# Expert weights in 16 KB rows, and a tail that joins, normalises and stores one token tile at a time

## What is computed

```python
# x: 264 tokens x 1024; h = rmsnorm(x)
logits = xt @ w_router + b_router
top_vals, top_idx = lax.top_k(logits, TOP_K)          # 4 of 32 experts a token
gates = jax.nn.softmax(top_vals, axis=-1)
...
gate, up = jnp.split(xb @ w_gate_up[e] + b_gate_up[e], 2, axis=-1)   # 1024 -> 2 x 1024
gate = jnp.minimum(gate, SWIGLU_LIMIT)
up = jnp.clip(up, -SWIGLU_LIMIT, SWIGLU_LIMIT)
act = gate * jax.nn.sigmoid(SWIGLU_ALPHA * gate) * (up + 1.0)
y = act @ w_down[e] + b_down[e]                                      # 1024 -> 1024
...
x = x + sum over a token's 4 experts of gates * y
y = rmsnorm(x, norm_final)
```

## Time and profile before

| | |
|---|---|
| median of 3 runs | 1428.51 us (1427.23 to 1429.93) |
| the profiled execution: time | 1428.02 us |
| its span | 1426.0 us |
| TensorE busy | 1331.8 us, 93% |
| VectorE, ScalarE, GpSimd busy | 374.5, 248.6, 60.4 us |
| moved | 515 MB in 84,586 packets, 361 GB/s over the span |

### The profile page before, as it was taken

The page is one execution under the profiler, slowest core; times in us unless marked ns, Lnnn a source line. Parts: engine busy times, 40 slices in busy tenths (PEclk is TensorE's granted clock), DMA queues, the critical chain, the costliest instruction groups (busy, mean ns, idle before and its releaser), DMA issues.

```text
span 1426.0 us, 19764 instructions
## 1 busy us (share of the span) xinstructions
PE 1331.8 (93%) x7729; PEld 632.0 (44%) x7729; DVE 374.5 (26%) x836; ACT 248.6 (17%) x403; POOL 60.4 (4%) x101
## 2 busy tenths in 40 slices
PE   6999959979996999999999999999999999999995
PEld 5666547647753433433343333333343333333333
DVE  3001684221225222212222222122221222212223
ACT  2010212220214111111111111111111111111112
POOL 2022220210000000000000000000000000000000
PEclk9999979989998999999999999999999999999998
DMA  9998574376883799999999999999999999999993
GB/s 341 371 360 333 192 264 179 121 255 245 319 359 136 302 424 422 421 421 422 422 422 421 422 422 422 423 421 423 422 422 422 422 423 422 422 421 423 422 422 121
DMA packets 84586, 515.13 MB, mean 361 GB/s; under 512 B 8451, under 2 KB 9563, under 8 KB 34608
## 3 DMA queue, kind: packets, MB, share of 16 engines
q1 hardware_dynamic: 77648, 493.69, 85.5%
q0 software_dynamic: 6576, 20.25, 4.4%
q10 hardware_dynamic: 336, 0.82, 0.2%
HBM read 511.21 MB, written 47.52 MB: 392 GB/s over the span
## 4 chain that ended last, share of the span: by engine, by line
PE 65%; DMA 20%; DVE 6%; SPq 6%; issue 2%; ACT 1%; POOL 0%; DVEq 0%; ACTq 0%
PE psum L573 61%; DMA weights<-in_w_gate_up 19%; SPq L445 5%; PE psum L576 4%; DVE qk L1384 1%; DMA weights<-in_w_mem_kv 1%; DMA weights<-in_cache_mem_kv 1%; DVE weights L1085 1%; DVE samp L1089 0%; DVE weights L1081 0%; DVE samp L1083 0%; DVE pair L1229 0%; ACT th L1539 0%; POOL weights L516 0%; DVE x L1409 0%
## 5 line engine op out<-in xcount | busy, mean ns | idle before, releaser
L573 PE MATMUL psum<-weights,wsp 128*64 128x512 f32 x2048 | 491.8, 603 | 15.0 <-DMA weights<-in_w_gate_up 14.3
L573 PE MATMUL psum<-weights,merged 128*64 128x512 f32 (+2 forms) x1152 | 272.8, 595 | 1.5 <-issue 1.5
L573 PEld LDWEIGHTS psum<-weights,wsp 128*64 128x64 f32 x2048 | 127.3, 136 | 267.1 <-issue 176.9
L1354 DVE TENSOR_TENSOR hT<-psum,hT 128x264 f32<-128x264 f32 x264 | 101.8, 428 | 529.6 <-PE psum L573 529.5
L573 PE MATMUL psum<-hT,weights 128*128 128x264 f32 x704 | 164.8, 391 | 1.2 <-DVE pair L1229 0.9
L573 PEld LDWEIGHTS psum<-weights,merged 128*64 128x64 f32 (+2 forms) x1152 | 89.6, 140 | 156.4 <-issue 148.3
L573 PEld LDWEIGHTS psum<-hT,weights 128*128 128x128 f32 x704 | 133.4, 191 | 28.8 <-DVE pair L1229 4.5
L1600 ACT COPY bT<-psum 128x264 f32<-128x264 f32 x33 | 12.5, 380 | 484.2 <-PE psum L576 484.2
L573 PE MATMUL psum<-bT,merged 64*128 64x264 f32 x528 | 94.2, 434 | 1.1 <-ACT merged L1619 0.7
L1384 DVE TENSOR_SCALAR qk<-psum,lowest 128x512 f32<-128x512 f32 x64 | 48.1, 751 | 162.7 <-PE psum L573 159.2
L573 PEld LDWEIGHTS psum<-bT,merged 64*128 64x128 f32 x528 | 39.8, 184 | 106.7 <-issue 103.9
(11 more groups left out here) (267 smaller groups left out, 721.9 us busy)
## 6 DMA issues: line engine op xcount, KB each, us to landing
weights<-in_w_gate_up SPq DMA_DIRECT2D x256, 1024.0 KB, 26.2
weights<-in_w_down SPq DMA_DIRECT2D x128, 1024.0 KB, 25.0
out<-in_cache_win_kv SPq DMA_DIRECT2D x8, 4094.0 KB, 20.9
weights<-in_w_in SPq DMA_DIRECT2D x13, 2048.0 KB, 12.5
out<-in_cache_win_kv SPq DMA_DIRECT2D x2, 4088.0 KB, 19.1
weights<-in_cache_mem_kv POOLq DMA_DIRECT2D x14, 512.0 KB, 6.4
weights<-in_cache_win_kv POOLq DMA_DIRECT2D x42, 128.0 KB, 4.5
weights<-in_w_mem_kv SPq DMA_DIRECT2D x2, 2048.0 KB, 18.0
```

The lines of the kernel that those rows point to most:

```text
L573: return nc.tensor.matmul(out, lhsT, rhs, start=start, stop=stop, **kw)
L1354: V.tensor_tensor(acc[:, c, :], p_a[j % 2][part], acc[:, c, :], ALU.add).then_inc(s_acc, 1)
```

## The change

Three things, all in the expert stage and behind it:

- A slot is 2 MB and there are six of them. Chunks 0 to 3 are 256 rows of w_gate_up (two neighbouring rows of 8 KB a partition), chunks 4 and 5 are 512 rows of w_down (four neighbouring rows of 4 KB a partition). A partition gets 16 KB in one piece. SyncE's waits and TensorE's `s_used` follow: one per slot.
- With it the gather takes its 128 stationary columns at a step of 2 (bf16), and the turns of h at a step of 4 (f32).
- The last expert is not scattered into `acc`. `acc` is turned into PSUM by f32 matmuls against the identity (`turn_sums`), and the last expert's rows are added on top, gate values as the stationary operand and `y_tok` as the moving one (`last_expert`). Three PSUM areas hold the three tiles. Join, square, root, scaling and store are done for each tile by itself, and ScalarE makes a first square root right after the loop. The counters of the loop drop the odd 33rd step.

```diff
-CHUNKS = KD + KD // 2
+GU, DN = 4, 2
+CHUNKS = GU + DN
+SLOT = 4 * D
...
-            return k if k < 4 else 4 + (k - 2) % 8
+            return k if k < 2 else 2 + (k - 1) % 4
...
-            return weights_at[:, n * 2048:(n + 1) * 2048]
+            return weights_at[:, n * SLOT:(n + 1) * SLOT]
...
             def chunk_dyn(e, k):
                 s = chunk_slot(k)
-                if k < KD:
-                    src = I["w_gate_up"][0, bass.ds(e, 1), k * P:(k + 1) * P, :].rearrange("e p c -> p (e c)")
-                    dst = chunk_view(k)
+                if k < GU:
+                    src = I["w_gate_up"][0, bass.ds(e, 1), k * 2 * P:(k + 1) * 2 * P, :].rearrange("e (p j) c -> p (e j c)", p=P)
                 else:
-                    r = (k - KD) * 2 * P
-                    src = I["w_down"][0, bass.ds(e, 1), r:r + 2 * P, :].rearrange("e (p j) c -> p (e j) c", p=P)
-                    dst = chunk_view(k).rearrange("p (j c) -> p j c", j=2)
-                sp.dma_start(dst, src).then_inc(s_chunk_in[s], 16)
+                    src = I["w_down"][0, bass.ds(e, 1), (k - GU) * 4 * P:(k - GU + 1) * 4 * P, :].rearrange("e (p j) c -> p (e j c)", p=P)
+                sp.dma_start(chunk_view(k), src).then_inc(s_chunk_in[s], 16)
...
-                    sp.wait_ge(s_job, last_job[{6: 17, 8: 18, 10: 19, 4: 20}[chunk_slot(k) // 2 * 2]])
+                    sp.wait_ge(s_job, last_job[{3: 17, 4: 18, 5: 19, 2: 20}[chunk_slot(k)]])
...
                     if k == CHUNKS - 1:
-                        sp.wait_ge(s_y, n33 + 1)
-                    elif k == KD - 1:
+                        sp.wait_ge(s_y, n32)
+                    elif k == GU - 1:
                         sp.wait_ge(s_gu, n32 * 2)
-                    elif k < KD:
+                    elif k < GU:
                         sp.wait_ge(s_used, n32 * USED + (k + 1 - USED))
                     else:
                         sp.wait_ge(s_used, n32 * USED + (k - USED))
                     chunk_dyn(e, k)
...
-                    ks, out = slice(k * P, (k + 1) * P), p_x[:, k * SLOTS:(k + 1) * SLOTS]
+                    first = k // 2 * 2 * P + k % 2
+                    ks, out = slice(first, first + 2 * P - 1, 2), p_x[:, k * SLOTS:(k + 1) * SLOTS]
...
-                        pe.wait_ge(s_chunk_in[chunk_slot(k)], n32 * 16 + 16)
-                        w = chunk_view(k)
+                        if k % 2 == 0:
+                            pe.wait_ge(s_chunk_in[chunk_slot(k // 2)], n32 * 16 + 16)
+                        w = chunk_view(k // 2)[:, (k % 2) * 2 * D:(k % 2 + 1) * 2 * D]
...
-                        if k < KD - 1:
+                        if k % 2 == 1 and k < KD - 1:
                             last.then_inc(s_used, 1)
...
-                            first = k // 2 * 2 * P + k % 2
-                            last = turn(p_hT[:, k, :], h_tok[:, first:first + 2 * P - 1:2], P)
+                            first = k // 4 * 4 * P + k % 4
+                            last = turn(p_hT[:, k, :], h_tok[:, first:first + 4 * P - 3:4], P)
...
-                        c = KD + k // 2
+                        c = GU + k // 4
...
-                        if k % 2 == 0:
+                        if k % 4 == 0:
                             pe.wait_ge(s_chunk_in[chunk_slot(c)], n32 * 16 + 16)
-                        w = chunk_view(c)[:, (k % 2) * D:(k % 2 + 1) * D]
+                        w = chunk_view(c)[:, (k % 4) * D:(k % 4 + 1) * D]
                         last = column_pair(p_y, actT[:, k, :], w[:, 0:512], w[:, 512:1024], k == 0, k == KD - 1)
                         if k == KD - 1:
                             last.then_inc(s_y, 1)
-                        elif k % 2 == 1:
+                        elif k % 4 == 3:
                             last.then_inc(s_used, 1)
-                last33 = b * (E + 1) + E
-                pe.wait_ge(s_ytok, last33 + 1)
-                pe.wait_ge(s_gT, last33 + 1)
-                for j in range(PAIRED):
-                    scatter(last33, j)
...
-            pe.wait_ge(s_accout, 1)
-            for t, (t0, tn) in enumerate(TILES):
-                w = wide[t % 2]
-                if t == 2:
-                    pe.wait_ge(s_finT, 1)
+            joined = (psum[:, 0:1024], psum[:, 1024:2048], wide[1])
+            def turn_sums(t):
+                t0, tn = TILES[t]
                 for k in range(KD):
-                    last = turn(w[0:tn, k * P:(k + 1) * P], acc[:, k, t0:t0 + tn], P)
-                last.then_inc(s_finj, 1)
+                    mm(joined[t][0:tn, k * P:(k + 1) * P], acc[:, k, t0:t0 + tn], ident, k % 4 == 0, False, skip_group_check=True)
+            def last_expert(t):
+                t0, tn = TILES[t]
+                mm(joined[t][0:tn, 0:512], gT[0:SLOTS, t0:t0 + tn], y_upper, False, True, skip_group_check=True)
+                mm(joined[t][0:tn, 512:1024], gT[SLOTS:2 * SLOTS, t0:t0 + tn], y_lower, False, True,
+                   skip_group_check=True).then_inc(s_finj, 1)
+            pe.wait_ge(s_accout, 1)
+            turn_sums(0)
+            turn_sums(1)
+            pe.wait_ge(s_ylast, 1)
+            last_expert(0)
+            last_expert(1)
+            turn_sums(2)
+            last_expert(2)
...
-            for t, (_, tn) in enumerate(TILES):
+            def join(t):
+                tn = TILES[t][1]
                 dve.wait_ge(s_finj, t + 1)
-                V.tensor_tensor(x1[0:tn, t, :], x1[0:tn, t, :], wide[t % 2][0:tn, :], ALU.add).then_inc(s_finT, 1)
-            rms_scale(stat[:, 28:31], D, 14)
-            dve.wait_ge(s_rt, 6)
-            seq(V.reciprocal(stat[:, 28:31], stat[:, 28:31]))
-            dve.wait_ge(s_gfin_in, 16)
-            for t, (_, tn) in enumerate(TILES):
+                V.tensor_tensor(x1[0:tn, t, :], x1[0:tn, t, :], (psum[:, 0:1024], psum[:, 1024:2048], wide[1])[t][0:tn, :],
+                                ALU.add).then_inc(s_finT, 1)
+            def root(t):
+                rms_scale(stat[:, 28 + t:29 + t], D, 12 + t)
+            def finish(t):
+                tn = TILES[t][1]
+                dve.wait_ge(s_rt, 6 + t)
+                seq(V.reciprocal(stat[:, 28 + t:29 + t], stat[:, 28 + t:29 + t]))
                 V.scalar_tensor_tensor(x1[0:tn, t, :], x1[0:tn, t, :], stat[0:tn, 28 + t:29 + t], gfin[0:tn, :], ALU.mult,
                                        ALU.mult).then_inc(s_fin, 1)
+            join(0)
+            join(1)
+            root(0)
+            join(2)
+            root(1)
+            dve.wait_ge(s_gfin_in, 16)
+            finish(0)
+            root(2)
+            finish(1)
+            finish(2)
...
-                    act.wait_ge(s_y, n33 + 2)
+                    act.wait_ge(s_y, n32 + 1)
                     A.copy(y_tok, p_y).then_inc(s_ytok, 1)
+                act.wait_ge(s_ytok, b * E + (E + 1))
...
-            for t, (_, tn) in enumerate(TILES):
+            act.sem_inc(s_ylast, 1)
+            A.activation(stat[:, 39:40], stat[:, 39:40], ACT.Sqrt)
+            def square(t):
+                tn = TILES[t][1]
                 act.wait_ge(s_finT, t + 1)
                 squares(stat[0:tn, 28 + t:29 + t], x1[0:tn, t, :], xr[0:tn, t, :])
-            act.wait_ge(s_ms, 6)
-            A.activation(stat[:, 28:31], stat[:, 28:31], ACT.Sqrt).then_inc(s_rt, 1)
+            def root(t):
+                act.wait_ge(s_ms, 6 + t)
+                A.activation(stat[:, 28 + t:29 + t], stat[:, 28 + t:29 + t], ACT.Sqrt).then_inc(s_rt, 1)
+            square(0)
+            square(1)
+            root(0)
+            square(2)
+            root(1)
+            root(2)
```

More of the change, by code:

```diff
@@ L190, in sem @@
             return ctx.enter_context(nc.semaphore(name))
-        weights_at = sb("weights", [P, CHUNKS * 2048])
-        scratch = weights_at[:, 0:4 * 2048]
-        ring = weights_at[:, 4 * 2048:CHUNKS * 2048]
+        weights_at = sb("weights", [P, CHUNKS * SLOT])
+        scratch = weights_at[:, 0:2 * SLOT]
+        ring = weights_at[:, 2 * SLOT:CHUNKS * SLOT]
         def block_view(name, p=P):
@@ L469, in _ @@
             with sp.Fori(1, E) as e:
[L470 removed]
+                one_expert(e, e)
             sp.wait_ge(s_done["posm"], 1)
@@ L868, in gather, with scatter @@
                 last.then_inc(s_gath, 1)
-            def scatter(n33, j):
+            def scatter(n32, j):
                 if j >= 2:
-                    pe.wait_ge(s_acc, n33 * KD + 2 * (j - 1))
+                    pe.wait_ge(s_acc, n32 * KD + 2 * (j - 1))
                 cs = slice(j * P, (j + 1) * P)
@@ L910, in one_pass @@
                                 last.then_inc(s_gu, 1)
-                        if k < KD - 1:
+                        if k % 2 == 1 and k < KD - 1:
                             last.then_inc(s_used, 1)
                         if k == 1:
-                            pe.wait_ge(s_ytok, n33 + 1)
-                            pe.wait_ge(s_gT, n33 + 1)
+                            pe.wait_ge(s_ytok, n32 + 1)
```

(26 more changed lines are left out.)

37 lines of the change are left out of this document (15 added, 22 removed).

## The result

| | before | after |
|---|---|---|
| median | 1429.21 us (1427.23 to 1429.93, 4 runs) | 1410.23 us (1409.70 to 1411.58, 4 runs) |
| the profiled execution: time | 1428.02 us | 1409.84 us |
| its span | 1426.0 us | 1408.0 us |
| packets | 84,586 | 56,939 |

The ratio of the times is 0.9876, with a 95% interval of 0.9858 to 0.9893. The two spans differ by 18.0 us, the forecast was 11.1. Three stretches of the span show where that comes from. Their bounds are the first and the last copy of y_tok, since each starts as soon as a down product ends.

What follows compares the result with a forecast made beforehand. Transfers were taken to bound the late experts (29.82 us each against TensorE's 28.31). Terms -14.2 + 2.2 + 0 + 0.9 = -11.1 us, from 1428.02, gave 1417 us; own range 1411 to 1423, outer range 1410 to 1431.

Steps and rivals of the forecast that it cites:

- What bounds the kernel: Expert stage: TensorE needs 28.31 us an expert, weight transfers set 29.82 once the starting stock is eaten, around expert 14.
- Rows of 16 KB, -14.2: Weight transfers: 9.9 ns a row, so fewer, larger rows give 429 GB/s and 29.34 us an expert, -14.2 us.
- The rival of an unchanged rate: Weight transfers: a limit behind the rows keeps the rate at 422 GB/s, time 1431.1 us; chance 0.11.
- that of a third of the row cost: Weight transfers: the skill's packet cost of 3.5 ns holds, gain about 5 us, time 1426 us; chance 0.06.
- Larger slots, +2.2: End of the expert stage: TensorE ends 4.5 us behind the last landing instead of 2.3, +2.2 us once.
- Startup, 0 give or take 1.5: First experts with six slots: expert 1's weights complete about 503.5 us, as before; 0, give or take 1.5 us.
- The steps, 0: Stationary loads of gather (step 2, bf16) and turns (step 4, f32): no dearer than before, 0 us.
- Both rivals that slowed TensorE down: Expert stage loads: turns slowed, 1424.5 us, chance 0.07; gather slowed, 1455.5 us at twice as long, chance 0.08.
- The tail, +0.9: Down product's end to span's end: 24.6 us instead of 23.7, the 3.9 us loop exit following the down product.
- 24 at 0.238 us: Tail, turn_sums(0) and (1): 24 of 32 instructions at half clock, 8 at 0.153 us, together 6.9 us.
- The range's lower end for this term, -3: Tail: low case of -3 us, where TensorE leaves the loop in 2 us and keeps its clock, 32 x 0.153.

Runs made afterwards that it cites:

- experiment 3: The changed kernel, still six transfers of 2 MB per expert, but each partition's 16 KB come as two rows of 8 KB; 1424.13 us, ratio to before 0.9966.
- experiment 4: The changed kernel with its slots filled in rows of 4 KB, 10 transfers per expert; 1454.44 us, ratio to before 1.0187.
- Experiment 5: The changed kernel with one wait more: TensorE waits for the last y_tok copy before leaving the loop; 1414.71 us, ratio to before 0.9920.
- experiment 6: The changed kernel with each tile's last_expert straight behind its turn_sums, VectorE and ScalarE following the tiles; 1411.11 us, ratio to before 0.9891.
- experiment 7: The kernel of experiment 6 with only VectorE's order changed, to that in which its inputs arrive; 1408.89 us, ratio to before 0.9879.
- experiment 1: The kernel before with the change's six 2 MB slots, 16 KB rows and steps, but the old tail; 1418.07 us, ratio to before 0.9924.

## Why the prediction came out as it did

The sign was right. The median of 1410.23 us lies in the range of 1410 to 1431, by 0.2 us, and outside the forecast's own 1411 to 1423; two of the four runs are below 1410. So it was luck that the range held it. The spans differ by 18.0 us where the sum had 11.1, and nearly all of that is one term, the tail. Term by term:

- **What bounds the kernel: right.** Two lines, TensorE's 28.3 us an expert and the transfers' slower pace; the cheaper transfer shortened the late experts only. The change of pace came between experts 13 and 14, where it was put.
- **Rows of 16 KB, -14.2: right.** 30 periods x (29.82 - 29.36) = -13.8, at 429 GB/s; by the landings of the last chunks of experts 1 and 31 (505.41 and 1399.88 us before, 505.33 and 1386.26 now) it is -13.5. Experiments 3 and 4 show the mechanism: the cost goes with the number of rows, and it is 9.4 to 9.6 ns where 9.9 was read. The rival of an unchanged rate and that of a third of the row cost are gone.
- **Larger slots, +2.2: right in kind, small by 0.3.** TensorE ends 4.9 instead of 4.5 us behind the last landing (by the landings 2.4 before), +2.5. The missing part is in the sum: 4.89 + 5.02 + 4.72 + 7.47 + 6.92 is 29.0 us, not 28.9, and the copy starts 0.2 us later still, which gives a lag of 4.8. The waits are at chunks 0 and 1, as forecast, 0.2 and 0.7 us.
- **Startup, 0 give or take 1.5: within its bounds.** The stage's -10.1 is -13.5 + 2.5 and a remainder of +0.9. Against the first copy, expert 1 is complete that much later (10.6 us behind it, for 9.7). The forecast's 503.5 us for that landing was 1.9 early for both kernels, which cancels. Behind rows of 8 KB, experiment 3 shows 2.1 us (4.5 less the lag's 2.4).
- **The steps, 0: right.** The loads take 0.56 and 1.83 us, and early copies are 28.32 us apart. Both rivals that slowed TensorE down are gone. The Trainium skill ("SBUF — State Buffer", section "Door 1: The DMA port swizzle"), cited for one of them, wants two accesses in a line of 16 bytes for full speed, and these loads, with one, take as long as before; the other half of that passage, which names a step of 4 f32 as free, agrees with the row.
- **The tail, +0.9: wrong, -6.9.** The step that failed is "TensorE's way out of the loop, 3.9 us of idle now, comes straight behind the down product", and with it "24 at 0.238 us": half clock because of that idle time. The 3.9 us of the earlier trace rows were what was left over of an exit of 4.3 to 4.8 us, most of it one jump, that starts when the sequencer is through with its last wait, not behind the last matmul. Before, that last wait was for VectorE's adds, with 0.7 us of work behind it. The change took the scatter away, so the last wait is for the last chunk of weights, and with slots of 2 MB 4.9 us of matmuls are left behind it. The idle time is 0.56 us, the clock stays at 1.00, and turns of tiles 0 and 1 take 3.84 instead of 6.9 us. That is 3.4 and 3.1 us of the 7.8 by which the term was wrong; of the rest, 0.9 are TensorE's last steps (4.8 us for 5.7). Full clock was priced too high as well: 0.153 us an instruction, where the 32 take 0.12. The range's lower end for this term, -3, supposed an exit of 2 us and a full clock, and even so it was too high.

Experiment 5 confirms the failed step from the other side: with a wait put behind the down product, the tail is 23.0 us, near the 24.6 forecast, though made up otherwise (5.2 us of idle time and 5.5 of turns, for 3.9 and 6.9). The part that a sum of parts can't show is the interaction: larger slots cost 4.5 us in the stage at 8 KB rows, and hand 3.4 back in the tail.

## What to carry to other kernels

Idle time on "issue" behind a loop is not a fixed price: find the last wait of the engine ahead of the exit, ask how much queued work lies behind it, and look for the jump among the sequencer's records. Where the exit can run beside matmuls that need no more waits, it costs little (0.13 to 0.56 us here), and TensorE keeps its clock for what follows. When transfers set the pace, count rows, not transfers (here with rows of 4 to 16 KB in transfers of 1 and 2 MB), and read the price of a row from two stretches of one's own trace with different row sizes. When an engine's work is split by tiles, every engine in the chain needs the order in which its inputs arrive; reordering one of them alone can lose what it gains, as experiments 6 and 7 show.

## What the runs showed of the hardware

- From the read of the flag to the first matmul behind the jump TensorE takes 4.3 to 4.8 us, in all nine kernels; 3.38 to 3.85 us of it are one jump, during which one transfer of 16 KB of instructions is seen. Queued matmuls run on meanwhile. The last branch of the loop takes 0.08 us, VectorE's jump on the same flag 0.06.
- A row costs 9.4 to 9.6 ns on top of its bytes, from 4 to 16 KB; halving the number of transfers at equal rows changed nothing (422 GB/s both).
- The granted clock stayed at 1.00 over idle times of 0.4 to 0.6 us, and was 0.66 as the mean of the 5 us behind 2.2 and 5.2 us of idle time, part of them at 1.2 GHz and part at 2.4; in both cases 32 f32 matmuls of 128 columns took 5.47 us instead of 3.84. Behind 3.9 and 3.8 us of idle time (before, experiment 1) it was 0.50, so the longer idle time didn't bring the slower clock; what decides that these runs don't settle.
- f32 stationary loads at a step of 4 elements and bf16 ones at a step of 2 take the same time as at steps of 2 and 1 (0.56 us for four and 1.83 us for 56, for 0.55 and 1.82).
